# A three-branch transformer block on one core: another order for the beginning, and two chunks of the modulation loaded elsewhere

## The reference

```python
c_act = jax.nn.silu(c)
mod = (c_act @ mod_w[i] + mod_b[i])[:, None, :]
sh0, sc0, g0, sh1, sc1, g1, sh2, sc2, g2 = jnp.split(mod, N_MOD, axis=-1)
h = modulate(rms_norm(x, norm_g[i, 0]), sh0, sc0)      # h * (1 + sc0) + sh0
x = x + 0.5 * g0 * swiglu(h, ffn_w_gu[i, 0], ffn_w_down[i, 0])
...
def swiglu(h, w_gu, w_down):
    g, u = jnp.split(h @ w_gu, 2, axis=-1)
    return (jax.nn.silu(g) * u) @ w_down
```

## Time and profile before

| | |
|---|---|
| runs | 1356.36 us median of 3 (1356.36 to 1356.87) |
| profiled execution | 1355.27 us, its span 1353.6 us |
| granted clock | mean 0.996 |
| PE, DVE, ACT, POOL busy | 98%, 70%, 47%, 11% of the span |
| DMA | 226 GB/s over the span, 310 to 350 GB/s in the first 170 us |
| chain that ended last | PE 89%, DVE 4%, ACT 2%, DMA 2% |

### The profile page before, as it was taken

How to read it: one execution, slowest core, us unless ns; L and a number is a source line. 1 busy time by engine, 2 the same in 40 slices (tenths; PEclk the granted TensorE clock), 3 DMA queues, 4 the chain that set the end, 5 groups by cost and what they waited for, 6 DMA issues and landing times.

```text
span 1353.6 us, 17828 instructions
## 1 busy us (share of the span) xinstructions
PE 1322.1 (98%) x6262; PEld 1077.4 (80%) x6262; DVE 947.8 (70%) x1128; ACT 641.0 (47%) x847; POOL 151.8 (11%) x234
## 2 busy tenths in 40 slices
PE   5999999899999999999999999999999999999998
PEld 3678888788888888888878788888887778888886
DVE  3788888879888788887777665465786557554442
ACT  3344334454333643334666643435655654644442
POOL 3110001200001100000231100001026000000000
PEclk9999999999999999999999999999999999999999
DMA  9999988399887789875554386555545434465540
GB/s 325 333 350 333 310 294 280 124 344 312 304 300 231 269 286 334 302 261 182 193 170 125 126 291 205 186 187 193 167 145 195 157 124 160 142 225 188 188 169 31
DMA packets 186743, 305.92 MB, mean 226 GB/s; under 512 B 8661, under 2 KB 135045, under 8 KB 186553
## 3 DMA queue, kind: packets, MB, share of 16 engines
q1 hardware_dynamic: 165576, 224.63, 49.6%
q0 software_dynamic: 21104, 80.46, 17.0%
HBM read 303.99 MB, written 1.06 MB: 225 GB/s over the span
## 4 chain that ended last, share of the span: by engine, by line
PE 89%; DVE 4%; ACT 2%; DMA 2%; issue 1%; POOL 0%; POOLq 0%; SPq 0%; DVEq 0%; ACTq 0%
PE ps L526 27%; PE ps L528 27%; PE ps L527 27%; DVE wlo L1928 1%; PE ps L608 1%; PE ps L644 1%; DVE arena L1969 1%; DMA raw<-in_ffn_w_gu 1%; PE ps L635 1%; DMA arena<-in_mod_w 1%; PE ps L681 1%; ACT whi L1315 1%; PE ps L971 1%; PE ps L993 0%; PE ps L617 0%
## 5 line engine op out<-in xcount | busy, mean ns | idle before, releaser
L1928 DVE TENSOR_TENSOR wlo<-raw,whi 128x2048 fp32r<-128x2048 f32 x212 | 481.6, 2295 | 96.3 <-ACT whi L1315 88.5
L526 PE MATMUL ps<-whi,nthi 128*128 128x512 f32 (+1 forms) x1264 | 506.2, 400 | 5.0 <-DVE ntlo L2368 1.8
L528 PE MATMUL ps<-whi,ntlo 128*128 128x512 f32 (+1 forms) x1264 | 493.5, 390 | 0.0
L527 PE MATMUL ps<-wlo,nthi 128*128 128x512 f32 (+1 forms) x1264 | 492.5, 390 | 0.0
L1315 ACT ACTIVATE whi<-raw 128x2048 fp32r<-128x2048 f32 x212 | 397.5, 1909 | 80.0 <-DMA raw<-in_ffn_w_gu 29.3
L526 PEld LDWEIGHTS ps<-whi,nthi 128*128 128x128 f32 x1264 | 238.5, 189 | 54.3 <-issue 5.7
L528 PEld LDWEIGHTS ps<-whi,ntlo 128*128 128x128 f32 x1264 | 238.3, 189 | 51.3
L527 PEld LDWEIGHTS ps<-wlo,nthi 128*128 128x128 f32 x1264 | 238.9, 189 | 45.2
L1969 DVE SCALAR_TENSOR_TENSOR arena<-arena,cact 128x512 f32<-128x512 f32 x238 | 178.8, 751 | 10.2 <-DMA arena<-in_mod_w 2.5
L526 PE MATMUL ps<-whi,hthi 128*128 128x512 f32 x440 | 172.9, 393 | 0.3 <-issue 0.3
L528 PE MATMUL ps<-whi,htlo 128*128 128x512 f32 x440 | 171.6, 390 | 0.0
(11 more groups left out here) (292 smaller groups left out, 868.0 us busy)
## 6 DMA issues: line engine op xcount, KB each, us to landing
raw<-in_ffn_w_gu SPq DMA_DIRECT2D x176, 512.0 KB, 5.2
arena<-in_mod_w POOLq DMA_DIRECT2D x72, 1024.0 KB, 6.6
raw<-in_ffn_w_down SPq DMA_DIRECT2D x88, 512.0 KB, 5.6
raw<-in_w_in SPq DMA_DIRECT2D x44, 512.0 KB, 4.6
raw<-in_w_gate_up SPq DMA_DIRECT2D x44, 512.0 KB, 4.9
raw<-in_diff_w_qkv SPq DMA_DIRECT2D x24, 512.0 KB, 4.6
raw<-in_w_down SPq DMA_DIRECT2D x22, 512.0 KB, 5.7
raw<-in_diff_w_o SPq DMA_DIRECT2D x8, 512.0 KB, 4.1
```

Source lines behind the costliest of these rows:

```text
L526: pe.matmul(o, hi, wh, start=start, stop=False)
L527: pe.matmul(o, hi, wl, start=False, stop=False)
L528: return pe.matmul(o, lo, wh, start=False, stop=stop)
L1928: v.tensor_tensor(wlo[:, s * PIECE:(s + 1) * PIECE], raw[:, r * PIECE:(r + 1) * PIECE], hi, ALU.subtract).then_inc(w_lo, 1)
```

## The change

In words:

- POOL loads each of the first four chunks in quarters of 512 KB with a semaphore each, and chunk 0's half ahead of chunk 2's. DVE's adds and PE's own products wait by quarters. Chunk 0's products are made in two halves (own_half), with turn_join of token block 0 between them. The sums of chunks 2 and 3 go into other banks (T and 0).
- keep_awake comes before the first products, with 36 transposes; the one behind the joins is gone.
- The first pieces of both halves (both_tokens) are multiplied for both token blocks with the high parts first: high x high, low x high, block 1's high x high, then high x low part, and so on, each with its own wait. ACT and DVE have their steps in another order to match; the four blocks of steps 0 and 1 are finished in another order too.
- Chunk 4 no longer waits for piece 4. Chunk 6 waits for piece 6, chunk 7 for piece 8 (before, chunk 5 waited for piece 6).
- Chunk 5 (MOD_SLOW) leaves the row of chunks: its halves are loaded into xn one after the other, the first behind chunk 8, the second ahead of chunk 11 and behind the fourth slow add; DVE adds its eighths one or two at a time behind the second to sixth step of the loop and the last two behind the loop, into gate. PE turns it behind the last step's turn_inner (turn_slow), DVE keeps it there.
- In first_head and step 2 ACT and DVE split piece 4 ahead of the first silu, and DVE splits piece 10 behind the second half of the chunk instead of ahead of it.

The diff, its core:

```diff
+        slow_half = xn[:, :].rearrange("p (k n) -> p k n", k=4)
+        slow_acc = gate[:, 0:MCH]
...
+        MOD_SLOW = (0, 5)
+        SLOW_STEPS = (1, 2, 3, 3, 4, 5, 6, 6)
+        MOD_STEP = [((0, 6),), ((0, 17),), ((1, 7),), ((1, 16),), ()]
...
-                    load_gu(gu, 0, 0, [(first_landed[2][1], 16)])
+                    load_gu(gu, 0, 0, [(first_landed[0][3], 16)])
                     load_gu(gu, 1, 0)
-                    load_gu(gu, 0, 4, [(first_landed[3][0], 16)])
+                    load_gu(gu, 0, 4, [(first_landed[3][1], 16)])
...
+            def turn_slow():
+                pe.wait_ge(slow_step, KT)
                 o = bank(M)
-                for k in range(KT):
-                    if k % 4 == 0:
-                        pe.wait_ge(first_landed[i][k // 4], 16 * lap)
+                for q in range(MCH // P):
+                    mm = pe.transpose(o[:, q * P:(q + 1) * P], slow_acc[:, q * P:(q + 1) * P], ident[:, :])
+                mm.then_inc(filled[M], 1)
+            def own_half(i, o, h):
+                for k in range(4 * h, 4 * h + 4):
+                    if k % 2 == 0:
+                        pe.wait_ge(first_landed[i][k // 2], 16)
                     mm = pe.matmul(o[0:1, :], cact[:, k:k + 1], mfirst[i][k // 4][:, k % 4, :],
                                    start=(k == 0), stop=(k == KT - 1))
-                    if k == 3:
-                        mm.then_inc(first_used, 1)
-                mm.then_inc(filled[M], 1)
+                mm.then_inc(filled[M] if h else first_used, 1)
...
+                def one(o, h, part, t, w, opens=False, closes=False):
                     for k in range(4):
+                        a = part[:, 4 * h + k, t * P:(t + 1) * P]
+                        mm = pe.matmul(o, a, w[:, k, :], start=(opens and k == 0), stop=(closes and k == 3))
+                    return mm
+                def both_tokens(h, o0, o1):
+                    p = n.next("piece").first
+                    wh, wl = (w[:, p * PIECE:(p + 1) * PIECE].rearrange("p (k n) -> p k n", k=4) for w in (whi, wlo))
+                    pe.wait_ge(w_hi, p + 2)
+                    pe.wait_ge(nt_hi, 2 * h + 1)
+                    one(o0, h, nth, 0, wh, opens=(h == 0))
+                    pe.wait_ge(nt_lo, 2 * h + 1)
+                    one(o0, h, ntl, 0, wh)
+                    pe.wait_ge(nt_hi, 2 * h + 2)
+                    one(o1, h, nth, 1, wh, opens=(h == 0))
+                    pe.wait_ge(w_lo, p + 2)
+                    mm = one(o0, h, nth, 0, wl, closes=(h == 1))
+                    if h:
+                        mm.then_inc(filled[T], 1)
+                    pe.wait_ge(nt_lo, 2 * h + 2)
+                    one(o1, h, ntl, 1, wh)
+                    one(o1, h, nth, 1, wl, closes=(h == 1)).then_inc(w_used, 1)
+                def half(o, t, h, w, ks=range(4)):
+                    for k in ks:
                         kk = 4 * h + k
                         mm = three(o, nth[:, kk, t * P:(t + 1) * P], ntl[:, kk, t * P:(t + 1) * P],
                                    w[0][:, k, :], w[1][:, k, :], kk == 0, kk == KT - 1)
                     return mm
-                w0 = views()
-                t0 = bank(T)
-                pe.wait_ge(nt_lo, 1)
-                half(t0, 0, 0, w0)
-                a = bank(A)
-                pe.wait_ge(nt_lo, 2)
-                half(a, 1, 0, w0).then_inc(w_used, 1)
-                own_chunk(1, 1)
+                t0, a = bank(T), bank(A)
+                both_tokens(0, t0, a)
+                o = bank(M)
+                own_half(1, o, 0)
+                own_half(1, o, 1)
                 w1 = views()
                 b = bank(B)
-                half(b, 1, 0, w1)
+                half(b, 1, 0, w1, (0, 1))
                 turn_row(gate[0:1, :])
-                sum_chunk()
+                sum_chunk(0)
+                half(b, 1, 0, w1, (2, 3))
                 m = bank(M)
                 half(m, 0, 0, w1).then_inc(w_used, 1)
-                w0 = views()
-                pe.wait_ge(nt_lo, 3)
-                half(t0, 0, 1, w0).then_inc(filled[T], 1)
+                both_tokens(1, t0, a)
                 w1 = views()
                 half(m, 0, 1, w1).then_inc(filled[M], 1)
                 turn_one(0, T, T)
-                pe.wait_ge(nt_lo, 4)
-                half(a, 1, 1, w0).then_inc(w_used, 1)
-                turn_one(1, M, M)
+                turn_one(1, A, A)
                 half(b, 1, 1, w1).then_inc(w_used, 1)
-                turn_one(0, A, A)
+                turn_one(0, M, M)
                 d0 = down_piece()
                 pe.wait_ge(drained[T], n.seen(T))
                 down_block(d0, 0, 0, True, False)
...
-                if f and gated is not None:
+                if f == 0:
+                    turn_slow()
+                elif gated is not None:
...
+            pe.wait_ge(ident_landed, 16)
+            keep_awake(T, 36)
             pe.wait_ge(cact_ready, 1)
-            own_chunk(0, 1)
+            own = bank(M)
+            own_half(0, own, 0)
+            turn_join((0,))
+            own_half(0, own, 1)
             pe.wait_ge(prm_landed, 16 * 9)
-            pe.wait_ge(ident_landed, 16)
             o = bank(A)
             pe.transpose(o[:, 0:NROWS], prow[0:NROWS, :], ident[0:NROWS, 0:NROWS])
             pe.transpose(o[:, 128:200], brow[0][:, :], ident[0:72, 0:72])
             pe.transpose(o[:, 256:328], brow[1][:, :], ident[0:72, 0:72]).then_inc(filled[A], 1)
             pe.wait_ge(consts_set, 3)
             turn_row(gate[0:1, :])
-            turn_join((0,))
-            sum_chunk()
+            sum_chunk(T)
             turn_join((1,))
-            keep_awake(T, 20)
             ffn(0, mod_cols(0, 2))
...
             def first_head():
                 split(1)
+                half_hi(0, 0)
                 act.wait_ge(xt_done, 3)
                 scaled_tiles(0, 1)
-                half_hi(0, 0)
                 half_hi(1, 0)
-                split(2)
+                split(1)
                 keep_row(gate[0:1, 0:BLK])
                 n.next(M)
                 split(1)
@@ -1520,15 +1557,14 @@
                 scaled_tiles(4, 2)
                 half_hi(0, 1)
                 half_hi(1, 1)
-                split(1)
+                split(2)
                 gated_half(0, full(T))
-                split(1)
-                gated_half(1, full(M))
+                gated_half(1, full_at(A, 2))
                 hidden_hi(0, 0, T)
-                gated_half(0, full_at(A, 2))
+                gated_half(0, full(M))
+                hidden_hi(0, 1, A)
+                gated_half(1, full_at(B, 3))
                 hidden_hi(1, 0, M)
-                gated_half(1, full_at(B, 3))
-                hidden_hi(0, 1, A)
                 split(1)
                 hidden_hi(1, 1, T)
                 split(4)
...
-                step(0, 0)
+                if f == 0:
+                    gated_half(0, full(A))
+                    gated_half(1, full_with_piece(B, 3))
+                    split(1)
+                    inner_hi(0)
+                else:
+                    step(0, 0)
...
                 scaled_tiles(0, 1)
-                split(1)
                 x_lo(0, (0,))
+                split(1)
                 x_lo(1, (0,))
                 split(1)
                 add_chunk(3)
-                split(2)
                 keep_own_chunk(chunk_at(*MOD_FIRST[1]))
-                keep_chunk(chunk_at(*MOD_FIRST[3]))
+                keep_chunk(chunk_at(*MOD_FIRST[3]), 0)
                 dve.wait_ge(drained[M], n.seen(M))
                 scaled_tiles(4, 2)
+                split(1)
                 x_lo(0, (1,))
                 x_lo(1, (1,))
                 split(1)
                 pass_by(T)
                 product(0, T)
+                n.next(A)
+                product(1, A)
+                split(1)
+                pass_by(M)
+                product(0, M)
+                hidden_lo(0, 0, T)
+                hidden_lo(0, 1, A)
                 c = add_chunk(halves=(0,))
-                pass_by(M)
-                product(1, M)
-                hidden_lo(0, 0, T)
-                split(1)
-                n.next(A)
-                product(0, A)
-                hidden_lo(1, 0, M)
-                add_chunk(halves=(1,), of=c)
                 n.next(B)
                 product(1, B)
-                hidden_lo(0, 1, A)
+                hidden_lo(1, 0, M)
                 split(1)
                 hidden_lo(1, 1, T)
-                split(1)
+                add_chunk(halves=(1,), of=c)
+                split(2)
                 keep_turned(chunk_at(*MOD_HEAD[0]))
-                c = add_chunk(halves=(0,))
-                split(1)
-                add_chunk(halves=(1,), of=c)
+            def slow_add(k):
+                if k % 4 == 0:
+                    dve.wait_ge(slow_landed[k // 4], 16)
+                if k == 0:
```

(43 more changed lines are left out.)

48 lines of the change are left out of this document (28 added, 20 removed).

## The result

The changed kernel took 1368.13 us in the median of 4 runs (1367.41 to 1371.88), the kernel before 1356.36 (1354.56 to 1356.87) on the same chip. The ratio is 1.0095, 95% interval 1.0074 to 1.0115: slower, by 11.8 us between the medians and 12.9 by the ratio. I had forecast 1357.5 and a range of 1348 to 1361.5.

The account below looks back on a forecast made before the run. PE, busy 98% of the span, was taken as the bound, with loads setting the pace before the mark. -0.65 (mark) + 1.7 (clock) + 0.1 = +1.15 us, so 1357.5 on the runs' median; range 1348 to 1361.5.

Parts of the forecast that it names:

- the mark: PE's start of turn_inner closing the first turn of FFN 0's loop, 110.92 us before; forecast 110.25, 0.65 us sooner.
- piece 9: Weights sharing the engines with chunk 7 ahead of step 2's silu; issued at 70.45, forecast to land at 80.0.
- piece 10: Weights DVE splits behind the second half of a chunk; forecast split by 93.9, freeing the slot for piece 13.
- piece 13: Weights ahead of the mark, issued at 94.0; forecast 102.5, bounds 99 and 105.6, giving the range -3.5, +3.1.
- Every sign that I named for the next profile: Early opening times, piece 4 after 50, DVE's piece 6 near 70, PE's wait of 3 us or more at the mark.
- The clock: Half clock after PE's long wait at the mark: 1.7 us of full-speed work lost behind it, where nothing hides them.
- The loop and the end: Loop steps of 17.3 us behind the mark: slow adds fit, chunk 11 issued at 168.2; +0.1 us in all.
- nothing lost: Chunk 11 behind POOL's wait for four slow adds: lands 175.7, adds must begin by 177.6, 1.9 us to spare.
- rival B: POOL's and SP's transfers share engines evenly, weights not held up; PE passes the mark 6.3 us early; 1351.9, chance 0.24.
- fits: DVE in the loop: some 15 us of a 17.3 us step used, so slow adds of 0.75 us fit, twice that in two places.
- D: Slower, ACT's queue before step 2's silu: piece 9 takes the full 11.6 us beside chunk 7; 1360.4, chance 0.26.
- C: Lead kept whole: PE passes the mark without a wait at 99.9, no clock loss behind it; 1345.5, chance 0.10.

Follow-up runs that it names:

- e1: Changed kernel with the slow chunk's second half loaded behind chunk 12 instead of ahead of chunk 11; 1356.82 us, ratio 1.0005 to the kernel before.
- e7: e1 with chunk 4 waiting for piece 4 to land, as in the kernel before; 1357.23 us, ratio 1.0009.
- e9: e6 with the slow adds earlier, one instead of three behind the loop's last turn; 1349.40 us, ratio 0.994.
- e2: e1 with chunk 5 neither loaded nor summed, its sum set to zero; 1353.70 us, ratio 0.9974.
- e4: Kernel before, with GpSimd waiting ahead of chunk 11 until VectorE has split piece 23, so chunks 11 and 12 are held; 1364.66 us, ratio 1.0056.
- e10: Changed kernel, wait for four slow adds kept, chunk 11's second half and chunk 12's halves each held until pieces 26, 27, 28 land; 1361.92 us, ratio 1.0048.
- e6: e5 with chunk 8's halves loaded only when pieces 13 and 14 have landed; 1351.65 us, ratio 0.9964.
- e5: e1 with the slow chunk's first half loaded behind chunk 10 instead of chunk 8, its adds later; 1354.05 us, ratio 0.998.
- e3: e1 with chunk 7 loaded only when piece 11 has landed and chunk 8 only when piece 13 has; 1357.61 us, ratio 1.0017.

## Why the prediction was wrong

**Right up to the mark, in part by luck.** Forecast and measured: chunk 0 done 18.95 and 17.9, modc 21.75 and 21.35, first weights 25.15 and 24.32, chunk 1 done from 37.8 and 37.2, mark 110.25 and 109.93. In between errors cancelled: DVE was through with piece 6 at 71.8 and not 70.35; piece 9 came at 75.1 and not 80.0, since it landed ahead of chunk 7, and the delay met pieces 11 and 12 instead, which ACT had at 91.37 and 96.74. DVE was through with piece 10 at 90.4 and not 93.9, so piece 13 was issued earlier than forecast, but took longer; ACT had it at 102.18, where I had 102.5. So PE waited 10.0 us at one place (and 0.8 at another) where I had 5.5 and 2.8. That most of the lead is lost there was right; that the mark agrees to 0.3 us is luck, since the same code met it 3 us earlier in e1. Every sign that I named for the next profile lay ahead of the mark or right behind it, so none of them could warn of what follows.

Two slips in the working carry nothing: 1 MiB at 372 GB/s takes 2.82 us and not 2.85, and 36 transposes at half speed from 4 us on end at 12.5 and not 12.

**The clock** term was 1.7 and measured 2.5 us. That is within its scatter: in the nine profiles that have one long wait at the mark and none in the step behind it, that step costs 1.4 to 2.7 us over 17.29, and not by the length of the wait (10.2 us cost 1.4 in e7, 4.1 us cost 2.7 in e9).

**The step that failed: "The loop and the end", "nothing lost".** I had POOL released at 167.4 (168.03) and asked only whether chunk 11 lands before 177.6. It did: DVE began it at 177.06. But I stopped at the next instruction behind the wait, and the term had no range of its own: the forecast's range came from piece 13 and the rivals. Chunk 12 stood behind the same wait, and had been free to go from 157 to 161 (e1); I priced neither its place in the burst nor the weights that share the engines with it. The term is 8.3 us in the profile instead of 0, with 1.6 of the 2.3 us in the step behind it (the other 0.75 are the slow adds, e1 and e2). I had the number for it at hand: 4.5 against 11.6 us, which I used for the weights ahead of the mark alone. e1 takes the term away, and e4 makes it without the change. In the changed kernel it is made of starved weights, as ACT's waits for the gu loads and the absence of a PE wait for a chunk's sum show; e10 shows that with the burst spread late chunks come to cost something too.

The Trainium skill, DMA: Bandwidth & Descriptors, section Queues, rings and completion order, has each DMA engine alternate between queues packet by packet. I read that in rival B as a fair share and set it against the 11.6. The trace agrees with the rule (707 packets to 705), and not with my reading: with packets of 3.8 and 1.0 KB, even turns starve the weights.

**A slow add "fits".** It does in a step of 17.3 us; in the shorter ninth step it cost 0.75 us.

**The rivals.** D had the sign, but not the mechanism: piece 9 wasn't late. B and C did not happen; e6 and e9 show that a good part of C's lead can be kept once chunk 8 and the slow half leave the stretch ahead of the mark. What stays open: how many bytes ahead of the mark cost how much (e5's profile doesn't show its gain), why the same code meets the mark at times 3 us apart (in e4, 2.3 us later than in the kernel before, 113.25 and 110.92), and what sets the clock's price behind a wait.

## What to carry to other kernels

When a wait is put into a queue, list everything that will stand behind it and when each would have gone, not only the next instruction: the price is the later burst as well as the delay, and the burst is paid by whoever shares the engines. Load by need: a lead won at the beginning is only kept if the transfers that aren't needed yet are held until those that are have landed, and held ones must come back in a place with room (e3 against e6). A load that waits for something late belongs at the end of its queue's row, behind the loads that are free to go.

## What the runs showed of the hardware

Two DMA queues that both had work shared the engines evenly by packets: 707 to 705 from 178 to 187 us in the changed kernel, and 696 to 692 in the same stretch of e4. By bytes that was 3.8 to 1 (2.70 and 0.71 MB) and 3.9 to 1 (2.72 and 0.69 MB). In e1 POOL's loads were not bunched, the engines stood idle for a part of the same 9 us, and the gu loads issued there took 5.0 us in the median.

PE stood idle from 99.9 to 109.9 us in the changed kernel. The granted clock was 1.00 up to 104 us, 0.50 (the lower of the two levels, 1.2 GHz) from 106 to 114, while PE was first idle and then busy, and 1.00 again from 116.
